# Expert rows taken up between the query units of a routed feed-forward, instead of behind them

## The reference

```python
def block(xb):                                     # 128 tokens, twice
    q = (xb @ w_q).reshape(128, 8, 2, 128)         # 8 heads, two halves each
    scores = einsum('thpd,hpkd->thpk', q, sub_keys)
    top_s, top_i = lax.top_k(scores, 16)           # 16 of 128 in either half
    cand_s = top_s[:, :, 0, :, None] + top_s[:, :, 1, None, :]   # 256 candidates
    best_s, best_pos = lax.top_k(cand_s, 16)       # 16 experts per head and token
    gate = softmax(best_s)
    act = gelu(einsum('thkd,td->thk', u[expert], xb))
    return einsum('thk,thkd->td', gate * act, v[expert])
```

## Time and profile before

| | |
|---|---|
| time, median of 3 runs | 2068.43 us (2066.64 to 2073.89) |
| the profiled execution | 2074.13 us, of which the span from first to last instruction 2072.3 us |
| granted TensorE clock, mean | 0.967 of full speed |
| PE busy | 1863.2 us (90%) |
| DVE busy | 1310.5 us (63%) |
| ACT busy | 918.8 us (44%) |
| gathers (software queue) | 38368 packets, 274.74 MB |

### The profile page before, as it was taken

How to read it: one execution, slowest core, us unless ns; L and a number is a source line. 1 busy time by engine, 2 the same in 40 slices (tenths; PEclk the granted TensorE clock), 3 DMA queues, 4 the chain that set the end, 5 groups by cost and what they waited for, 6 DMA issues and landing times.

```text
span 2072.3 us, 29851 instructions
## 1 busy us (share of the span) xinstructions
PE 1863.2 (90%) x11656; PEld 1498.1 (72%) x11656; DVE 1310.5 (63%) x2389; ACT 918.8 (44%) x1876; POOL 315.5 (15%) x340
## 2 busy tenths in 40 slices
PE   7999899999999999999999988889987777778777
PEld 7999879999999999779999878788332322223222
DVE  5555775655655652776556766666877777776444
ACT  4444464444444431464444443544544443444343
POOL 1000101000100000001000000132433333333330
PEclk9999999999999987999999899999999999999999
DMA  7555417955455533214555232346999999999997
GB/s 270 184 184 179 136 62 144 314 183 184 157 188 187 187 106 144 82 34 161 185 187 187 76 129 102 120 162 238 423 421 421 421 421 422 421 422 421 421 422 317
DMA packets 96971, 488.35 MB, mean 236 GB/s; under 512 B 10640, under 2 KB 10896, under 8 KB 63808
## 3 DMA queue, kind: packets, MB, share of 16 engines
q0 software_dynamic: 38368, 274.74, 34.4%
q1 hardware_dynamic: 58464, 211.70, 30.1%
HBM read 482.21 MB, written 4.19 MB: 235 GB/s over the span
## 4 chain that ended last, share of the span: by engine, by line
PE 60%; DMA 23%; DVE 10%; ACT 4%; issue 2%; POOL 0%; SPq 0%; ACTq 0%; POOLq 0%; DVEq 0%
PE PS L484 16%; PE PS L486 16%; PE PS L485 16%; DMA raw<-uv,A 6%; DMA XF<-uv,A 5%; DMA WL<-uv,A 5%; PE PS L2015 3%; DVE WL L922 2%; DMA XL<-uv,A 2%; DMA WH<-uv,A 2%; DMA YH<-uv,A 2%; DMA XH<-uv,A 2%; DMA YL<-uv,A 1%; PE PS L1497 1%; DVE A L1217 1%
## 5 line engine op out<-in xcount | busy, mean ns | idle before, releaser
L484 PE MATMUL PS<-XH,WH 128*128 128x256 f32 x2176 | 631.7, 290 | 39.4 <-DVE WL L922 15.8
L486 PE MATMUL PS<-XH,WL 128*128 128x256 f32 x2176 | 622.5, 286 | 0.0
L485 PE MATMUL PS<-XL,WH 128*128 128x256 f32 x2176 | 622.4, 286 | 0.0
L922 DVE TENSOR_TENSOR WL<-raw,WH 128x1024 fp32r<-128x1024 f32 (+1 forms) x379 | 446.5, 1220 | 91.7 <-ACT WH L590 90.7
L484 PEld LDWEIGHTS PS<-XH,WH 128*128 128x128 f32 x2176 | 421.5, 194 | 47.2 <-issue 32.5
L590 ACT ACTIVATE WH<-raw 128x1024 fp32r<-128x1024 f32 (+1 forms) x390 | 386.9, 1042 | 94.7 <-PE PS L486 69.8
L485 PEld LDWEIGHTS PS<-XL,WH 128*128 128x128 f32 x2176 | 422.2, 194 | 0.2
L486 PEld LDWEIGHTS PS<-XH,WL 128*128 128x128 f32 x2176 | 421.6, 194 | 0.0
L876 ACT ACTIVATE A<-A,RTK 128x1 f32<-128x1 f32 x256 | 75.3, 294 | 332.1 <-DVE A L1466 328.5
L532 POOL TENSOR_TENSOR A<-hT 128x256 f32<-128x256 f32 x64 | 56.3, 904 | 954.2 <-DVE hT L966 732.4
L484 PE MATMUL PS<-GH,WH 128*128 128x256 f32 x704 | 198.1, 281 | 0.0
(11 more groups left out here) (302 smaller groups left out, 2670.8 us busy)
## 6 DMA issues: line engine op xcount, KB each, us to landing
raw<-wst SPq DMA_DIRECT2D x388, 512.0 KB, 4.4
raw<-wst SPq DMA_DIRECT2D x9, 384.0 KB, 3.3
vscr<-A POOLq DMA_DIRECT2D x1, 3072.0 KB, 35.8
A<-vscr POOLq DMA_DIRECT2D x1, 2048.0 KB, 21.9
C<-cst SPq DMA_DIRECT2D x1, 1236.5 KB, 10.7
raw<-uv,A POOLq DMA_INDIRECT x68, 32.6
hT<-xin SPq DMA_DIRECT2D x2, 512.0 KB, 5.1
A<-vscr POOLq DMA_DIRECT2D x1, 1024.0 KB, 11.8
```

Of the source, the lines that this page charges most:

```text
L484: pe.matmul(o, wh, xh, start=start, stop=False, skip_group_check=True)
L485: pe.matmul(o, wh, xl, start=False, stop=False, skip_group_check=True)
L486: return pe.matmul(o, wl, xh, start=False, stop=stop, skip_group_check=True)
L922: dv.tensor_tensor(WL[:, m % SPL, 0:w], raw[:, i % RAW, 0:w], f32(WH[:, m % SPL, 0:w]), ALU.subtract).then_inc(s_lo, 1)
```

## The change

MIX0 = 6: from query unit 6 on, two slots are done behind each unit by ACT and PE (slots 0 and 1 behind unit 6, up to 18 and 19 behind unit 15), and DVE does the dot products of unit n-1's slots behind its subtraction for unit n. The rest of the slots, 20 to 255, follow as before.

- PSUM: the output of block 0 moves to banks 6 and 7, so products and scores now share banks 0 and 1 in turn (`bank_q`, `bank_s`), with waits on ACT's copies to match; block 1 gets banks 0 and 1. `by_token` goes through bank 6.
- Homes: a home has a slot number from which it may be used. Slot g takes the home that was used longest ago among those allowed. Worked out from the code, the homes of slots 0 to 24 are: 0 to 4 YH, YL, ROW0, ROW1, XF; 5 to 8 YH, YL, ROW0, ROW1 again; 9 a raw pair; 10 to 12 XF, YH, YL; 13 a raw pair; 14 to 16 ROW0, ROW1, raw; 17 a raw pair; 18 to 22 XF, YH, YL, raw, ROW0; 23 a raw pair; 24 ROW1. Slots 25 to 30 take XH, XL and the places in WH and WL. From there each home comes round after 15 slots.
- PE no longer waits for the reciprocal root at unit 3; `by_token` stands behind unit 4, and the residual of block 0 (`begin(0)`) behind unit 5.
- Gates: the first two heads are done one at a time, with an Exp on ACT behind unit 4 and another behind unit 9. Choosing in the slot loop is four slots later.

```diff
-        YB = (0, 6)
+        YB = (6, 0)
+        def mixed(n):
+            return (2 * (n - MIX0), 2 * (n - MIX0) + 1) if n >= MIX0 else ()
+        MIXED = 2 * (16 - MIX0)
...
+        for k in sorted(range(4), key=lambda k: max(last[2 * k], last[2 * k + 1])):
+            m = max(last[2 * k], last[2 * k + 1])
+            rows.append((flat(raw[:, 2 * k:2 * k + 2, :]), (s_lo, m + 1), 2 * (m - PQ0 - MIX0) + 5))
+        over = 2 * (16 - MIX0) + 5
+        rows += [(flat(w[:, :, :]), (s_used, U("pq", 15)), over) for w in (XH, XL)]
+        rows += [(flat(w[:, 2 * k:2 * k + 2, :]), (s_used, U("pq", 15)), over) for w in (WH, WL) for k in range(2)]
...
+        for g in range(256):
+            n = min((n for n in range(SLOTS) if rows[n][2] <= g), key=lambda n: taken[n][-1] if taken[n] else -1)
+            before.append(taken[n][-1] if taken[n] else None)
...
 POOL
-                    po.wait_ge(s_y, g - SLOTS + 1)
+                    po.wait_ge(s_y, before[g] + 1)
...
 ACT, in the loop over the query units
                 ac.wait_ge(s_used, U("pq", n))
...
+                ac.activation(QP[:, n % QN_RING, :], PS[:, bank_q[n], 0:T], ACT.Copy).then_inc(s_qp, 1)
...
+                if n == 4:
+                    shares(0, 0, 1)
+                if n == 9:
+                    shares(0, 1, 1)
+                for g in mixed(n):
+                    slot(g)
...
 DVE
+            shares(0, 0, 1)
             for n in range(5, 16):
                 dv.wait_ge(s_hi, m + 1)
                 dv.tensor_tensor(WL[...], raw[...], f32(WH[...]), ALU.subtract).then_inc(s_lo, 1)
+                if n == 6:
+                    gates(0, 0, 1)
+                    route(0, 1, 0)
...
+                for g in mixed(n - 1):
+                    slot(g)
...
 PE, in the loop over the query units
+                elif scored(n - 1):
+                    pe.wait_ge(s_qp, n)
...
                 if n == 3:
-                    by_token(7)
                     pe.wait_ge(s_txf, 1)
-                    pe.wait_ge(s_rtk, 3)
...
+                if n == 4:
+                    by_token(7)
+                if n == 5:
+                    pe.wait_ge(s_rtk, 3)
+                    begin(0)
+                for g in mixed(n):
+                    slot(g)
+            pe.wait_ge(s_scr, 16)
+            begin(1)
+            for g in range(MIXED, 256):
+                slot(g)
```

More of the change, by code:

```diff
@@ L236 @@
 QN_RING = 6
+MIX0 = 6
 ARENA = 17024
@@ L469, in program, with scored @@
         x_cols = flat(hT[:, :, :])
+        def scored(n):
+            return (0,) if n == 1 else (n // 2 - 1,) if n % 2 == 0 and n >= 4 else (7,) if n == 15 else ()
+        def mixed(n):
+            return (2 * (n - MIX0), 2 * (n - MIX0) + 1) if n >= MIX0 else ()
+        MIXED = 2 * (16 - MIX0)
+        CHOOSING, GATES = {}, {(0, 0): 1, (0, 1): 2}
+        later = []
+        for blk in range(2):
+            for h in range(0, 8, 2):
+                if blk or h:
+                    GATES[blk, h] = len(GATES) + 1
+                    later += [("route", blk, hh, k) for hh in (h, h + 1) for k in range(6)]
+                    later += [("shares", blk, h, 2), ("gates", blk, h, 2)]
+        for n, what in enumerate(later):
+            CHOOSING[4 + 2 * n] = (what,)
+        GATE_AT = {16 * (8 * blk + h): n for (blk, h), n in GATES.items()}
         last = {}
@@ L852, in shares, with slot @@
                 ac.activation(bd, bd, ACT.Exp, scale=RTK[:, blk:blk + 1]).then_inc(s_bde, 1)
[L854 to L870, removed]
+            def slot(g):
                 blk, s = g // 128, g % 128
@@ L887, in act_program @@
                     ac.activation(OT[0], flat(PS[:, YB[0]:YB[0] + 2, :]), ACT.Copy).then_inc(s_ot, 1)
+            for n in range(16):
+                hi("pq", n)
+                ac.wait_ge(s_used, U("pq", n))
+                if n >= QN_RING:
+                    ac.wait_ge(s_scm, (n - QN_RING) // 2 + 1)
+                ac.activation(QP[:, n % QN_RING, :], PS[:, bank_q[n], 0:T], ACT.Copy).then_inc(s_qp, 1)
+                for h in scored(n):
+                    ac.wait_ge(s_scm, h + 1)
+                    for blk in range(2):
+                        ac.activation(flat(SC[blk][:, 2 * h:2 * h + 2, :]), PS[:, bank_s[h], 256 * blk:256 * blk + 256],
+                                      ACT.Copy).then_inc(s_scr, 1)
+                if n == 1:
+                    root(7)
+                if n == 4:
[6 more added lines that the diff above has]
+                slot(g)
             ac.wait_ge(s_left, 1)
@@ L892, in program @@
         FILL_DST = [(QB, 0.125), (QB, 0.125), (KB, 1.0), (KB, 1.0)] + [(G16, 1.0)] * 8
[L895 to L908, removed]
         def dve_program(dv):
@@ L1463, in dve_program @@
                         gates(*what[1:])
-                u = rows[g % SLOTS][0][:, 0:1024]
-                dv.wait_ge(s_g[g % SLOTS], 16 * (g // SLOTS + 1))
+                u = rows[home[g]][0][:, 0:1024]
+                dv.wait_ge(s_g[home[g]], 16 * turn_of[g])
                 dv.tensor_tensor_reduce(out=u, in0=f32(u), in1=XT[blk], scale=1.0, scalar=0.0, op0=ALU.mult, op1=ALU.add,
                                         accum_out=AV[:, blk, s:s + 1]).then_inc(s_dot, 1)
+            for k in range(6):
+                route(0, 0, k)
+            rstd(7)
+            by_token(2)
+            shares(0, 0, 1)
+            for n in range(5, 16):
+                m = PQ0 + n
+                i = spl_unit[m]
+                dv.wait_ge(s_hi, m + 1)
+                dv.tensor_tensor(WL[:, m % SPL, :], raw[:, i % RAW, :], f32(WH[:, m % SPL, :]), ALU.subtract).then_inc(s_lo, 1)
+                if n == 6:
+                    gates(0, 0, 1)
+                    route(0, 1, 0)
+                if n == 7:
+                    route(0, 1, 1)
+                for g in mixed(n - 1):
+                    slot(g)
+                if n == 8:
+                    route(0, 1, 2)
+                if n == 9:
+                    for k in range(3, 6):
+                        route(0, 1, k)
+                    shares(0, 1, 1)
+                if n == 11:
+                    gates(0, 1, 1)
+            for g in range(MIXED - 2, 256):
+                slot(g)
             dv.wait_ge(s_y, 256)
@@ L1967, in pe_program, with begin, slot @@
                     [(s_m2, 5 + k) for k in range(4)] + [(s_h, H0[6] + k + 1) for k in range(4)])
+            def begin(blk):
+                for kc in range(8):
+                    pe.matmul(PS[:, YB[blk] + kc // 4, 128 * (kc % 4):128 * (kc % 4) + 128],
+                              hT[:, kc, 128 * blk:128 * blk + 128], c("ident"), start=kc % 4 == 0, stop=False,
+                              skip_group_check=True)
+            def slot(g):
+                blk, s = g // 128, g % 128
+                pe.wait_ge(s_g[home[g]], 16 * turn_of[g])
+                pe.wait_ge(s_dg, g + 1)
+                v = f32(rows[home[g]][0][:, 1024:2048])
+                for q in range(2):
+                    ins = pe.matmul(PS[:, YB[blk] + q, :], DG[:, g % 4, :], v[:, 512 * q:512 * q + 512], start=False,
+                                    stop=s == 127, skip_group_check=True)
+                    if g == 255 and q == 0:
+                        ins.then_inc(s_left, 1)
+                ins.then_inc(s_y, 1)
             for n in range(16):
```

43 lines of the change are left out of this document (22 added, 21 removed).

## The result

| | before | after |
|---|---|---|
| time, median of 6 runs each | 2070.74 us (2066.64 to 2074.11) | 2086.68 us (2082.34 to 2088.11) |
| ratio | | 1.0072, 95% interval 1.0055 to 1.0089 |
| the profiled execution | 2074.13, span 2072.3 | 2087.15, span 2085.3 |
| granted TensorE clock, mean | 0.967 | 0.965 |

The change makes the kernel slower, by 0.7%, and the interval lies clear of 1. In the profiled executions it is 13.0 us.

A forecast was written before the change was run, and what follows sets the result against it. Bound by PE's query units, then by gathers alone, with unit 15's end between: 50.0 us delay less 39.8 for sixteen rows, plus 4.0 for the clock, is +14.2; from the median 2068.43, 2082.6 us, 8-in-10 range 2068 to 2093.

The forecast's parts named there:

- 18 slots and nine stops: Ahead of unit 15's product: 18 slots cost PE 31.0 us, waits for ACT's diagonal behind units 6 to 14 10.1 and 6.7.
- residual of block 0: Behind unit 5 on PE: block 0's residual, on no path before, now adds 1.95 us.
- table switches: ACT at units 6 and 9: Gelu and Exp table loads with PE waiting add 4.2 us together.
- half clock: Behind the long stops at units 6 and 9: PE drops to 1.2 GHz, losing 2.0 us each, 4.0 together.
- front: Units 3 to 5: without the reciprocal-root stop on PE, unit 5 starts near 1398.6 instead of 1402.54, gaining 3.9 us.
- given back by sixteen rows: Gathers: sixteen more rows issued ahead of unit 15's end save 16 x 2.49 us, 39.8 us.
- The event: End of unit 15's product frees XH, XL, WH and WL; XH's gather near 1489 us, 25 gathers ahead, 2.49 us a row behind.
- Late rows: PE's slots: DVE or POOL hold gathers back, each wait adding 3 to 5 us; 2090 with two; chance 0.04.
- Hidden stops: Slots behind the units: PE's waits for ACT shrink to about 0.5 us or none; 2066 or 2057.6 us; chance 0.10.
- about even: PE ahead of unit 15's end: stops and tables cost only 11 to 17 us, clock full; 2069 to 2074.6; chance 0.11.
- Clock down with the rhythm: PE in the query units: nine stops each leave half clock, 15 us more, 2098 us; chance beyond 2092 0.12.
- Dearer tables: ACT's table switches with PE waiting: each of three costs as much again, 3.9 us more, 2086.5 us; chance 0.03.

The follow-up runs named there:

- e2: The changed kernel with the first Gelu table loaded early, behind unit 5, and unit 9's Exp moved behind that unit's slots; 2078.56 us, 1.0036 of before.
- e4: The changed kernel with one edit on PE alone: the slots of unit n-1 stand behind unit n; 2057.33 us, 0.9945 of before.
- e3: The changed kernel with one slot behind each unit instead of two, 15 gathers ahead of unit 15's end instead of 25; 2092.76 us, 1.0121 of before.
- e7: The changed kernel with PE's slots one unit later and mixing begun at unit 4 instead of 6; 2055.62 us, 0.9950 of before.
- e1: The changed kernel with no slots between the query units; shared banks, new front and gates one head at a time stay; 2066.72 us, 0.9989 of before.
- e5: The changed kernel with PE's slots one unit later and mixing begun at unit 5 instead of 6; 2057.51 us, 0.9948 of before.
- e6: The kernel before with unit 14's product computed six times, which only delays unit 15's end; 2080.81 us, 1.0062 of before.

## Why the prediction was right

The direction, the size and the place were right: 2082.6 us forecast from the median shown, 2086.68 measured; +14.2 us forecast for the profiled execution, +13.0 measured. Of the 4.1 us between the medians 2.3 are the kernel before itself, 2068.43 in three runs and 2070.74 in six. Point by point, in the terms of its sum:

| term, us of delay on PE | predicted | measured |
|---|---|---|
| 18 slots and nine stops | 31.0 + 6.7 + 10.1 = 47.8 | 48.0 |
| residual of block 0 | 1.95 | 1.78 |
| table switches | 4.2 | 1.43 + 3.04 = 4.5 |
| half clock | 4.0 | 3.9 |
| front | -3.9 | -4.2 |
| sum | 54.05 | 53.9 |
| given back by sixteen rows | -39.8 | -40.9 |
| net | +14.2 | +13.0 |

*Where the measured column is from.* The slots: a unit with scores takes 9.18 where it took 3.73, one without 8.02 where it took 2.84, so 5 x 5.45 + 4 x 5.18 = 48.0. The residual: 4.62 from copy 5 to copy 6, which was 2.84. Table switches: by the idle times (3.21 - 1.78 and 4.55 - 1.51, the short ones being those of e2). Clock: the rest of the distances from copy 6 to 7 (12.31) and 9 to 10 (13.21), 1.70 and 2.15; the total of e2, 8.3, leaves 3.8. The front: from unit 3's copy to unit 5's first matmul 7.54 us, before 11.75. The rows: 53.9 less 13.0, so this line and the net are one measurement.

*The event.* XH's gather went out at 1492.62. The forecast "near 1489 (1484 to 1500)" gives as its middle the sum without the clock; with the 4 us for it, 1492.5 were due. 25 gathers stood ahead of it, as forecast, with no transfer just ahead of it, and the rate behind it was 2.53 us a row over the whole stretch. The 2.49 from the steady rows leaves out what the stretch as a whole has besides; over sixteen rows this is worth 0.7 us, and with a difference of 0.4 at the ends of the two stretches it makes the 1.1 us by which the net came out better.

*The stops.* Idle times 1.5 and 1.8, then 3.1 at unit 6 and 4.4 at unit 9 were forecast; 1.51, 1.78, 3.21 and 4.55 are in the trace. Copies 8.0 apart were met (8.02). The "8.9" for the others was wrong in the text, not in the sum: its own terms, 3.73 of before + 3.44 + 2.02, make 9.2, and 9.18 was measured. e4 then took the stops away as such and got 16.5 us for them.

*The clock.* It fell behind the two long stops and behind none of the seven short ones; in e2 none of the nine, all short, lowered it. The 2.0 us each were 1.7 and 2.15. But that it would fall was less sure than the text has it: e3's first stop, as long, cost nothing, and its second, at unit 9, cost 2.8 (12.12 us to the next copy where 6.30 and the 3.04 of tables were due). Nor is a short stop safe: PE's 1.57 ahead of unit 5 in e7 was followed by half clock, the 1.56 at the same place in the changed kernel was not. That this term came out at 3.9 for 4.0 is in part luck.

*The front.* Unit 5 was to start near 1398.6 and started at 1398.37. PE's idle of 1.56 there is the one new wait, for DVE's subtraction behind the copy of the reciprocal root.

*What was said to cost nothing.* Shared banks: shown by e1, and with slots between the units by e4, where unit 9's copy starts 7.17 behind unit 8's, which is 3.73 and two slots of 1.72. Late rows: none of the changed kernel's stops is ended by a row, and where DVE waits for one, there is time in hand: the longest such wait ahead of the event, 4.15, ended at 1449.91, 17.5 us ahead of that slot's Gelu at 1467.45, and the one with the least time in hand, 3.42, ended at 1419.48, 9.3 us ahead of its Gelu at 1428.82. The DMA share in the query units was forecast near 0.7 and was 0.77.

*The rivals.* Hidden stops, and about even: the stops were there in full, and ACT's order gave PE no way around them. Clock down with the rhythm: seven short stops here and nine in e2, no half clock. Dearer tables: from the load at 1436.01 to its Gelu at 1438.92 are 2.91 us with PE waiting. The Trainium skill, "ScalarE: Activation LUTs", section "What ACT_TABLE_LOAD costs", adds a drain of 1.38 us to each load of 1.28; by that rule it would be 5.3, an estimate. The trace does not agree, with its 2.91, and no run here shows such a drain.

*What I did not see.* I took the stops as given by ACT's order and asked only what they cost. They are the second largest term of the sum, 16.8 of 50.0 us, and the forecast does not draw the conclusion that moving PE's slots by one unit removes them (e4).

## What to carry to other kernels

Work that is put between the steps of an engine that runs in order, to fill another engine's idle time, must be ready when its turn comes. If the engine that prepares it takes it up only behind something that waits for the step just ahead, every place of insertion pays the whole chain between the two engines, here 1.5 to 1.8 us of idle time for each unit, and fewer insertions in each place do not help. Put it one step later (e4: 28 us less delay for one edit). And where two stages meet at one event, price the change by that event: the delay of the event against the transfers that got ahead of it, here 2.5 us for each, and less once the transfers no longer keep up with their issue (e4).

## What the runs showed of the hardware that was not expected

- The same stop does not always lead to the same clock. An idle of 3.21 us ahead of the slot was followed by half clock in the changed kernel (3.60 for the slot) and by full clock in e3 (1.96). Both idles of 4.55 were followed by half clock (3.75). No idle of 1.51 or 1.78 was, in any of the kernels, but one of 1.57, ahead of unit 5 in e7, was: granted clock 0.52 for 3.4 us. At the same place e1 to e5 and the changed kernel stood idle for 1.56 or 1.57, behind the same work, and ran at full clock (0.36 for the first matmul, 0.55 in e7). So in these runs the length of the idle time does not settle whether the clock falls.
- A product's first matmul (128x256) directly behind a slot (128x512) stands 0.68 long in the trace, where it is 0.36 behind scores or the residual. Nothing is lost by it: the product's second matmul starts at 1415.49, 1.72 + 0.21 behind the slot at 1413.56, and 0.21 is what it is behind the residual too (1402.98 and 1403.19).
- When the DMA engines are nearly full ahead of the event, rows got ahead are worth less than their 2.53 us. e4 should have ended 16 x 2.53 - 25.6 = 14.9 us sooner and ended 12.6 sooner; e5 17.1 and 14.7; e7 16.6 and 13.8. In all three the dot product of XH's row started 9.8 to 10.0 us behind its gather, and 5.4 to 5.9 in the changed kernel, e2, e3 and e6, so the queue was not empty when the event came. Why the loss is 2.3 to 2.8 us and not the whole 4 us or more by which the row is later stays open.
- The stretch ahead of the query units took between 1380.70 and 1390.89 us in kernels whose work is the same up to there. It goes with the granted clock: PE was busy for 1317.4 us of the first 1391 before, at 0.96, and for 1305.2 of the first 1381 in e1, at 0.97, with all but the same count of matmuls (10236 and 10241). Single runs of the kernel before spread by a similar 10.6 us, and there too the time follows the clock: 2063.82 us at 0.976 and 2074.42 at 0.967. Why the clock is granted otherwise is open.
